# Middle stage's column products: three equal groups of frames, or 512, 512 and 128 with narrow matmuls between wide ones

## The chip, the cores and the metric

The kernel runs on one core of a Trainium2 chip. The metric is the device time of one execution in microseconds (us); lower is better. The core's engines work side by side and wait for each other by semaphores: TensorE (PE; its weight loads are shown apart as PEld), VectorE (DVE), ScalarE (ACT), GpSimd (POOL) and SyncE (SP), which here only issues DMAs. TensorE writes its sums to PSUM, eight banks of 512 float32 words in each of 128 partitions; DVE and ACT read them from there.

## The reference, cut to what matters

Two layers of a streaming encoder run for 1024 prompt frames and for 8 streams of 16 frames, T = 1152 frames together. Layer 0 is a gated linear recurrence. Between the layers its output projection, residual and LayerNorm give x (1152 x 1024). The second layer starts from x:

```python
def mla_queries(x, pos, w_in, q_norm_g, w_uq, w_uk):
    proj = jnp.einsum('btd,de->bte', x, w_in)      # 1024 -> 512 + 2048
    cq = rms_norm(proj[..., :Q_LORA], q_norm_g)    # Q_LORA = 512
    gate = proj[..., Q_LORA:]                      # used as o * silu(gate)
    ...
def shared_latent_kv(x, pos, w_dkv, kv_norm_g):
    kv = jnp.einsum('btd,de->bte', x, w_dkv)       # 1024 -> 256 + 64
```

The change is in how `proj` is computed. The matrix `w_in_b` has 512 + 2048 = 2560 columns, that is 20 tiles of 128: four of cq, sixteen of the gate.

## The kernel before, in words

float32 products are made from float32r operands in two parts: an operand is split into a high part (written by ACT, `round_high`, L104) and the rest (written by DVE, `round_low`, L109). A product is then three matmuls: high x low, low x high, high x high (`product`, L112 to L117). In the profile L115, L116 and L117 are these three matmuls for every stage of the kernel.

The middle stage (`middle_programs`, about 556 to 953 us) first finishes the first layer: for each of nine tiles of 128 frames, matmuls of 512 columns (`m_w`, `m_g`), a LayerNorm on DVE, eight transposes on TensorE (`turn_tile`, L1235), and the split of the turned tile into `act_h` (ACT) and `act_l` (DVE, semaphore `tl_done`, which starts at 1, so that tile t is there at t + 2). Then come the **column tiles**: for column tile i (i = 0 to 19, `NCOL`) 128 columns of `w_in_b` over all eight blocks of 128 inputs are the stationary operand, and the frames, `act_h` or `act_l`, are the moving one. A column tile is 3 groups of `TG` = 384 frames, each group 8 x 3 = 24 matmuls; so 72 matmuls of 384 columns for a tile and 1440 in all. Each group's sums stand in a bank of their own, 384 of its 512 words, and tile i uses banks 0 to 2 or 3 to 5 by turns (`pc`).

What sets the order around them:

- SP loads the float32 columns of tile i + 2 into `m_c_raw` (512 KB, L1127) once `c_done` has reached i + 1, that is once all matmuls of tile i are done. ACT makes `m_c_h` (`high_columns`), DVE makes `m_c_l` (`low_columns`, semaphore `cl_ready`), both buffers by turns of two.
- ACT reads the finished tile from PSUM: for the four cq tiles a Square (L1385) and a copy (L1386), for the gate tiles a Sigmoid (L1393), which DVE multiplies with the sums (L1509) and SP stores. TensorE may start tile i + 2 in the same banks after that (`columns_free`).
- The first two column tiles are begun before the last tile of frames is turned. Their order on TensorE is: tile 1's group 0, tile 0's group 0, `turn_tile(8)`, tile 0's groups 1 and 2, tile 1's groups 1 and 2. `c_done` is raised after group 2 of each: once for tile 0, once for tile 1. From tile 2 on, a tile's three groups follow each other.
- From gate tile 3 on, a transposition and a 128-frame product of the shared latent (`latent`, 24 matmuls of 320 columns, banks 6 and 7) follow each gate tile. After the last column tile the heads' programs (attention) follow on TensorE.

Of the kernel before, what the change touches and what calls it, by code (L numbers as in the profile page):

```python
# [9 lines left out]
ACT = mybir.ActivationFunctionType  # L10
# [5 lines left out]
KD = D // P  # L16
SEQ, NSEQ, SLEN, PAST = 1024, 8, 16, 1024
T = SEQ + NSEQ * SLEN
NT = T // P
NPB = SEQ // P  # L20
TG = 384
NTG = T // TG
# [9 lines left out]
BANK = 512  # L32


def flat(ap):
    return ap.rearrange("p a b -> p (a b)")
# [75 lines left out]
def product(nc, out, left, right, first, last):  # L112

    (lh, ll), (rh, rl) = left, right
    nc.tensor.matmul(out, ll, rh, start=first, stop=False)  # L115
    nc.tensor.matmul(out, lh, rl, start=False, stop=False)  # L116
    return nc.tensor.matmul(out, lh, rh, start=False, stop=last)  # L117

GLA_STEPS = ["V0", "V1", "K0", "C0", "S0", "SI", "O0", "K1", "C1", "S1", "O1", "OT0",
# [62 lines left out]
def rows_product(nc, bank, shared, i, t):  # L185

    gh, gl, _ = shared.tile_of(t)
    for h in range(2):
        cols = slice(h * BANK, (h + 1) * BANK)
        mm = product(nc, bank[:, h], (gh[:, i], gl[:, i]), (shared.w_h[i][:, cols], shared.w_l[i][:, cols]), i == 0, i == KD - 1)  # L190
    return mm
# [811 lines left out]
def middle_programs(nc, k, m, kept_at, heads):  # L1003
# [20 lines left out]
    cq_raw = Arena(nc, (cq_at, cq_at + 4 * 4 * T)).take("m_cq_raw", [4, T])  # L1024
# [21 lines left out]
    c_h = col.take("m_c_h", [2, KD, P], F32R)  # L1046
    c_l = col.take("m_c_l", [2, KD, P], F32R)
# [12 lines left out]
    sg = late.take("m_sg", [2, T])  # L1060
# [7 lines left out]
    bank = k.bank  # L1068

    def py(t):  # L1070

        b = (4, 0, 2, 6)[t] if t < 4 else (0, 2)[t % 2]
        return bank[:, b:b + 2]

    def pt(t):

        b = 6 if t and t % 2 == 0 else 4
        return bank[:, b:b + 2]

    def pc(i):  # L1080
        return bank[:, 3 * (i % 2):3 * (i % 2) + 3, 0:TG]

    w_loaded = [m.sem(f"m_w_loaded{i}") for i in range(nk)]
    g_loaded = [m.sem(f"m_g_loaded{i}") for i in range(2)]
# [18 lines left out]
    def columns_free(eng, i):  # L1103

        if i < NCQ:
            eng.wait_ge(cq_out, i + 1)
        else:
            eng.wait_ge(gate_out, i - NCQ + 1)
# [7 lines left out]
    def behind_gate(j):  # L1116

        t = j - 3
        return (t - 1 if 0 <= t - 1 < NPB else None), (t if 0 <= t < NT else None)
# [103 lines left out]
    @block.tensor  # L1223
    def _(pe):
        def turn_tile(t):

            pe.wait_ge(x_ready, t * 2 + 2)
            if t == 1:
                pe.wait_ge(tl_done, 2)
            elif t == 2:  # L1230
                pe.wait_ge(sum_done, 4)
            elif t > 2:
                pe.wait_ge(tl_done, t)
            for c in range(KD):
                last = nc.tensor.transpose(pt(t)[:, c // 4, (c % 4) * P:(c % 4 + 1) * P], x[t % 3][:, c * P:(c + 1) * P], k.ident[:])  # L1235
            last.then_inc(turned, 1)

        pe.sem_inc(y_done, 3)
        for t in range(3, NT):
            if t > 3:  # L1240
                pe.wait_ge(gl_ready, t - 3)
                pe.wait_ge(sum_done, t - 2 if t < 6 else t - 1)
            for kt in range(nk):
                last = rows_product(nc, py(t), sh, kt, t)
            last.then_inc(y_done, 1)
            if t < 7:
                turn_tile(t - 3)
            elif t == 7:
                turn_tile(4)
                turn_tile(5)  # L1250
            else:
                turn_tile(6)
                turn_tile(7)

        def columns(i, tg):

            cols = slice(tg * TG, (tg + 1) * TG)
            for kt in range(KD):
                mm = product(nc, pc(i)[:, tg], (c_h[:, i % 2, kt], c_l[:, i % 2, kt]),
                             (k.act_h[:, kt, cols], k.act_l[:, kt, cols]), kt == 0, kt == KD - 1)  # L1260
            if tg == NTG - 1:
                mm.then_inc(c_done, 1)

        pe.wait_ge(cl_ready, 2)
        pe.wait_ge(sum_done, 8)
        pe.wait_ge(tl_done, 4)
        columns(1, 0)
        pe.wait_ge(sum_done, 9)
        columns(0, 0)
        turn_tile(NT - 1)  # L1270
        pe.wait_ge(tl_done, 7)
        columns(0, 1)
        pe.wait_ge(tl_done, NT + 1)
        columns(0, 2)
        columns(1, 1)
        columns(1, 2)

        def column_tile(i):
            pe.wait_ge(cl_ready, i + 1)
            columns_free(pe, i - 2)  # L1280
            for tg in range(NTG):
                columns(i, tg)

        def spread_rows(tiles, b):

            for n, t in enumerate(tiles):
                mm = nc.tensor.transpose(bank[:, b, n * P:(n + 1) * P], sums[:, t * P:(t + 1) * P], k.ident[:])
            mm.then_inc(spread, 1)

        def latent(t):  # L1290
            if t == 0:
                pe.wait_ge(kvl_ready, 1)
            if t < 2:

                pe.wait_ge(spread_out, 2 + t)
            else:
                pe.wait_ge(tl_k, t - 1)
            for kt in range(KD):
                cols = slice(t * P, (t + 1) * P)
                mm = product(nc, bank[:, 6 + t % 2, 0:KV], (k.act_h[:, kt, cols], k.act_l[:, kt, cols]),  # L1300
                             (kvw_h[:, kt], kvw_l[:, kt]), kt == 0, kt == KD - 1)
            mm.then_inc(kv_done, 1)

        def turn_latent(t):
            b, par = bank[:, 6 + t % 2], t % 2
            pe.wait_ge(c_ready, t + 1)
            pe.wait_ge(kr_ready, t + 1)
            for c in range(2):
                nc.tensor.transpose(b[:, c * P:(c + 1) * P], cn[:, par, c * P:(c + 1) * P], k.ident[:])
            nc.tensor.transpose(b[:, 2 * P:3 * P], krn[:, par].rearrange("p a b -> p (a b)"), k.ident[:]).then_inc(turned_k, 1)  # L1310

        for i in range(2, NCQ):
            column_tile(i)
        for j in range(HEADS):
            column_tile(NCQ + j)
            if j == 0:
                pe.wait_ge(const_set, 3)
                pe.wait_ge(sums_step, NCQ - 1)
                for t in range(NT):
                    mm = nc.tensor.matmul(bank[:, 6, t:t + 1], sums[:, t * P:(t + 1) * P], ones[:], start=True, stop=True)  # L1320
                mm.then_inc(ss_done, 1)
            if j == 1:
                pe.wait_ge(rep_ready, 1)
                spread_rows(range(4), 7)
                spread_rows(range(4, 8), 6)
            if j == 2:
                pe.wait_ge(spread_out, 1)
                spread_rows(range(8, 9), 7)
            before, now = behind_gate(j)
            if before is not None:  # L1330
                turn_latent(before)
            if now is not None:
                latent(now)

    @block.scalar
    def _(act):
# [19 lines left out]
        def high_columns(i):  # L1356
            act.wait_ge(c_loaded[i % 2], 16 * (i // 2 + 1))
            if i >= 2:
                act.wait_ge(c_done, i - 1)
            round_high(nc, c_h[:, i % 2], c_raw[:, i % 2]).then_inc(ch_ready, 1)  # L1360
# [17 lines left out]
        def column_tile(i):  # L1378
            act.wait_ge(c_done, i + 1)
            if i < NCQ:  # L1380
                if i == 3:

                    act.wait_ge(sums_step, 1)
                dst = sums[:] if i == 0 else sg[:, i % 2]
                nc.scalar.activation(dst.rearrange("p (a b) -> p a b", a=3), pc(i), ACT.Square)  # L1385
                nc.scalar.copy(cq_raw[:, i].rearrange("p (a b) -> p a b", a=3), pc(i)).then_inc(cq_out, 1)  # L1386
            else:
                j = i - NCQ
                if j < 2:
                    act.wait_ge(sums_step, NCQ - 1)  # L1390
                else:
                    act.wait_ge(gate_stored[j % 2], 16 * (j // 2))
                nc.scalar.activation(sg[:, j % 2].rearrange("p (a b) -> p a b", a=3), pc(i), ACT.Sigmoid).then_inc(sig_done, 1)  # L1393
            if i + 2 < NCOL:
                high_columns(i + 2)

# [10 lines left out]
        for i in range(NCQ):  # L1407
            column_tile(i)
# [25 lines left out]
    def _(dve):  # L1434
# [69 lines left out]
        def column_tile(i):  # L1504
            if i >= NCQ:
                j = i - NCQ
                at = sg[:, j % 2].rearrange("p (a b) -> p a b", a=3)
                dve.wait_ge(sig_done, j + 1)
                nc.vector.tensor_tensor(at, pc(i), at, ALU.mult).then_inc(gate_out, 1)  # L1509
            if i + 2 < NCOL:  # L1510
                low_columns(i + 2)
# [41 lines left out]
        for i in range(NCQ):  # L1553
            column_tile(i)
# [1704 lines left out]
```

## Time and profile before

| | us |
|---|---|
| median of 3 runs | 1947.16 (1946.81 to 1948.17) |
| the profiled execution, its own time | 1946.45 |
| its span, first to last instruction | 1944.3 |
| busy in the span: PE / DVE / ACT / POOL | 1914.9 / 1061.8 / 768.6 / 394.0 |

A matmul's row in the trace gives its start and how long it took from there to its end. Matmuls overlap in their pipeline, so what a matmul costs TensorE is the step from its start to the next one's start, and not its duration. A row "x16" merges sixteen instructions: its duration reaches from the first start to the last end.

### The profile page before, as it was taken

Reading aid. Unit: us, or ns where it says so; the run is one execution under the profiler, and the core shown is the slowest. Engines: PE = TensorE matmul, PEld = TensorE weight load, DVE = VectorE, ACT = ScalarE, POOL = GpSimd, SP = SyncE. Lnnn points to the kernel's source line nnn. Section 1 sums busy time; section 2 is a strip of 40 time slices with the busy share of each in tenths; the row PEclk is TensorE's granted clock in tenths of the full one; section 3 lists DMA queues with packets and bytes.
Section 4 is the critical chain, followed back from the end, with each engine's and each line's share of the span. In section 5 each row is a group of like instructions: output and inputs, shape, how many; then the busy total and the mean of one; then the engine's idle time right before and its main releaser. Section 6 shows DMA issues by size and latency. Waiting matters only on the chain.

```text
span 1944.3 us, 31501 instructions
## 1 busy us (share of the span) xinstructions
PE 1914.9 (98%) x11771; PEld 1808.9 (93%) x11771; DVE 1061.8 (55%) x1943; ACT 768.6 (40%) x1346; POOL 394.0 (20%) x322
## 2 busy tenths in 40 slices
PE   9999999999999999999999999999999999999998
PEld 8999999999987999999999999999999989988886
DVE  4355446445658612422466676666666677753632
ACT  4333233233422221211455555555555567761100
POOL 0221222122311010000042432432433410000000
PEclk9999999999999999999999999999999999999999
DMA  6121122022236412233211112111111243363421
GB/s 183 34 78 55 35 67 78 27 62 68 79 117 201 128 44 69 80 107 104 89 34 50 41 50 63 34 54 56 38 49 42 73 135 92 96 226 136 157 87 43
DMA packets 186082, 158.55 MB, mean 82 GB/s; under 512 B 36144, under 2 KB 170544, under 8 KB 185744
## 3 DMA queue, kind: packets, MB, share of 16 engines
q1 hardware_dynamic: 180784, 139.60, 23.7%
q10 hardware_dynamic: 5040, 17.37, 2.6%
q8 instruction: 58, 0.95, 0.2%
q0 software_dynamic: 176, 0.43, 0.1%
q14 instruction: 24, 0.20, 0.0%
HBM read 115.52 MB, written 41.84 MB: 81 GB/s over the span
## 4 chain that ended last, share of the span: by engine, by line
PE 54%; DVE 7%; issue 5%; ACT 3%; DMA 1%; DVEq 0%; ACTq 0%; SPq 0%
PE ps L115 16%; PE ps L117 16%; PE ps L116 16%; PE ps L1925 1%; PE ps L1908 1%; PE ps L1907 1%; DVE h_pt_l L109 1%; ACT h_p L2041 1%; ACT h_p L2030 1%; DVE s_mx L2801 1%; DVE h_mx L2169 1%; DVE h_p L2126 1%; DVE h_p L2131 1%; DMA m_g_raw<-scratch_o 1%; DVE h_gate L2191 0%
## 5 line engine op out<-in xcount | busy, mean ns | idle before, releaser
L1821 POOL TENSOR_SCALAR h_p<-h_p,h_rsum 128x128 f32<-128x128 f32 (+7 forms) x128 | 220.7, 1725 | 442.8 <-DVE h_rsum L2173 442.8
L115 PE MATMUL ps<-act_h,a_w_l 128*128 128x384 f32 x768 | 270.8, 353 | 1.7 <-DVE a_w_l L109 1.7
L117 PE MATMUL ps<-act_h,a_w_h 128*128 128x384 f32 x768 | 260.1, 339 | 0.0
L116 PE MATMUL ps<-act_l,a_w_h 128*128 128x384 f32 x768 | 259.9, 338 | 0.0
L115 PE MATMUL ps<-act_h,m_c_l 128*128 128x384 f32 x480 | 162.9, 339 | 0.0
L117 PE MATMUL ps<-act_h,m_c_h 128*128 128x384 f32 x480 | 162.5, 339 | 0.0
L116 PE MATMUL ps<-act_l,m_c_h 128*128 128x384 f32 x480 | 162.5, 339 | 0.0
L115 PEld LDWEIGHTS ps<-act_h,a_w_l 128*128 128x128 f32 x768 | 144.2, 188 | 6.5 <-issue 3.3
L116 PEld LDWEIGHTS ps<-act_l,a_w_h 128*128 128x128 f32 x768 | 144.4, 188 | 3.3 <-issue 3.3
L117 PEld LDWEIGHTS ps<-act_h,a_w_h 128*128 128x128 f32 x768 | 144.1, 188 | 0.0
L104 ACT ACTIVATE h_pt_h<-ps 128x128 fp32r<-128x128 f32 (+2 forms) x192 | 87.1, 490 | 108.7 <-PE ps L1925 108.5
L109 DVE TENSOR_TENSOR h_pt_l<-ps,h_pt_h 128x128 fp32r<-128x128 f32 (+2 forms) x192 | 100.3, 551 | 47.8 <-ACT h_pt_h L104 47.8
L2041 ACT ACTIVATE h_p<-ps,h_mx 128x128 f32<-128x128 f32 (+7 forms) x128 | 94.8, 740 | 54.3 <-DVE h_mx L2169 54.0
L115 PE MATMUL ps<-o_w,o_g 128*128 128x512 f32 x288 | 112.4, 390 | 0.8 <-ACT s_olat L2677 0.8
L117 PE MATMUL ps<-o_w,o_g 128*128 128x512 f32 x288 | 112.1, 389 | 0.0
L116 PE MATMUL ps<-o_w,o_g 128*128 128x512 f32 x288 | 112.1, 389 | 0.0
L115 PE MATMUL ps<-cq_h,h_w_l 128*128 128x384 f32 x288 | 101.7, 353 | 0.6
L2169 DVE TENSOR_REDUCE h_mx<-ps 128x1 f32<-128x128 f32 (+7 forms) x128 | 97.0, 758 | 4.4
L117 PE MATMUL ps<-cq_h,h_w_h 128*128 128x384 f32 x288 | 96.5, 335 | 0.0
L116 PE MATMUL ps<-cq_l,h_w_h 128*128 128x384 f32 x288 | 96.4, 335 | 0.0
L115 PE MATMUL ps<-h_pt_h,h_v_l 128*128 128x256 f32 x320 | 92.3, 288 | 3.7 <-DVE h_gate L2191 3.0
L117 PE MATMUL ps<-h_pt_h,h_v_h 128*128 128x256 f32 x320 | 90.4, 283 | 0.0
(322 smaller groups left out, 4817.5 us busy)
## 6 DMA issues: line engine op xcount, KB each, us to landing
a_w_raw<-in_w_in_a SPq DMA_DIRECT2D x31, 512.0 KB, 4.1
m_c_raw<-in_w_in_b SPq DMA_DIRECT2D x20, 512.0 KB, 4.3
scratch_gate<-m_sg SPq DMA_DIRECT2D x16, 576.0 KB, 5.3
o_w_raw<-in_w_out_b SPq DMA_DIRECT2D x16, 512.0 KB, 6.3
h_gate<-scratch_gate SPq DMA_DIRECT2D x62, 128.0 KB, 2.0
scratch_og<-h_gate SPq DMA_DIRECT2D x62, 128.0 KB, 1.7
o_g_raw<-scratch_og SPq DMA_DIRECT2D x24, 256.0 KB, 4.3
a_xn<-in_x SPq DMA_DIRECT2D x9, 512.0 KB, 4.5
```

The source lines that it names most:

```text
L104: return nc.scalar.activation(high, x, ACT.Identity)
L109: return nc.vector.tensor_tensor(low, x, high.bitcast(F32), ALU.subtract)
L115: nc.tensor.matmul(out, ll, rh, start=first, stop=False)
L116: nc.tensor.matmul(out, lh, rl, start=False, stop=False)
L117: return nc.tensor.matmul(out, lh, rh, start=False, stop=last)
L1821: nc.gpsimd.tensor_scalar(weights_of(u), weights_of(u), rsum[:, u % PB], None, ALU.mult).then_inc(S["p_ready"], 1)
L1907: nc.tensor.matmul(out, rq[:, e, q], k.kr_l[:, kc], start=False, stop=False)
L1908: mm = nc.tensor.matmul(out, rq[:, e, q], k.kr_h[:, kc], start=False, stop=True)
L1925: mm = nc.tensor.transpose(bank[:, 4 + i % TB, j * P:j * P + P], p[:, u % PB, key * P:(key + 1) * P], k.ident[:])
L2030: last = nc.scalar.copy(rope_part(tg, 1)[b:b + 32], x[a:a + 32])
L2041: nc.scalar.activation(weights_of(u), scores_of(u), ACT.Exp, bias=mx[:, u % PB], accum_out=rsum[:, u % PB]).then_inc(S["exp_done"], 1)
L2169: nc.vector.tensor_reduce(mx[:, u % PB], scores_of(u), AX.X if n <= BANK else AX.XY, ALU.max, negate=True).then_inc(S["max_done"], 1)
```

## The change

The 1152 frames of a column tile are cut into 512, 512 and 128 instead of three times 384. The three banks then hold 1152 sums without holes (512, 512 and 128 words), and ACT and DVE read them as one run. The first group of 512 of a tile stands alone (24 matmuls). The second group of 512 and the group of 128 go side by side: for each input block and each of the three terms, first the matmul of 512 columns, then that of 128 columns with the same stationary operand. In the two tiles at the start, tile 1's second group goes side by side with the narrow groups of tile 0 and of tile 1: 512, 128, 128; and `c_done` is then raised by 2 at the end of this block. Two waits on `tl_done` ask for more turned tiles: 5 in place of 4 ahead of tile 1's group 0, and NT = 9 in place of 7 ahead of tile 0's group 1. The file gets 9 lines longer above this place, so that L1235 becomes L1244; the new matmuls are all L126.

```diff
+def products_beside(nc, parts, first, last):
+    for term in range(3):
+        for out, (lh, ll), (rh, rl) in parts:
+            mm = nc.tensor.matmul(out, lh if term else ll, rl if term == 1 else rh,
+                                  start=first and term == 0, stop=last and term == 2)
+    return mm
...
     def pc(i):
-        return bank[:, 3 * (i % 2):3 * (i % 2) + 3, 0:TG]
+        return flat(bank[:, 3 * (i % 2):3 * (i % 2) + 3])[:, 0:T]
...
-        def columns(i, tg):
-            cols = slice(tg * TG, (tg + 1) * TG)
+        def columns(*blocks):
             for kt in range(KD):
-                mm = product(nc, pc(i)[:, tg], (c_h[:, i % 2, kt], c_l[:, i % 2, kt]),
-                             (k.act_h[:, kt, cols], k.act_l[:, kt, cols]), kt == 0, kt == KD - 1)
-            if tg == NTG - 1:
-                mm.then_inc(c_done, 1)
+                parts = []
+                for i, tg in blocks:
+                    cols = slice(tg * BANK, min(tg * BANK + BANK, T))
+                    parts.append((pc(i)[:, cols], (c_h[:, i % 2, kt], c_l[:, i % 2, kt]),
+                                  (k.act_h[:, kt, cols], k.act_l[:, kt, cols])))
+                mm = products_beside(nc, parts, kt == 0, kt == KD - 1)
+            return mm
         pe.wait_ge(cl_ready, 2)
         pe.wait_ge(sum_done, 8)
-        pe.wait_ge(tl_done, 4)
-        columns(1, 0)
+        pe.wait_ge(tl_done, 5)
+        columns((1, 0))
         pe.wait_ge(sum_done, 9)
-        columns(0, 0)
+        columns((0, 0))
         turn_tile(NT - 1)
-        pe.wait_ge(tl_done, 7)
-        columns(0, 1)
+        pe.wait_ge(tl_done, NT)
+        columns((0, 1))
         pe.wait_ge(tl_done, NT + 1)
-        columns(0, 2)
-        columns(1, 1)
-        columns(1, 2)
+        columns((1, 1), (0, 2), (1, 2)).then_inc(c_done, 2)
         def column_tile(i):
             pe.wait_ge(cl_ready, i + 1)
             columns_free(pe, i - 2)
-            for tg in range(NTG):
-                columns(i, tg)
+            columns((i, 0))
+            columns((i, 1), (i, 2)).then_inc(c_done, 1)
```

The remaining lines of the diff take the `rearrange("p (a b) -> p a b", a=3)` off the operands of L1385, L1386, L1393 and L1509.

On TensorE, in the middle of any column tile from tile 2 on, there stands before (the names are moving and stationary operand):

```order
L115 MATMUL ps<-act_h,m_c_l 128x384
L116 MATMUL ps<-act_l,m_c_h 128x384
L117 MATMUL ps<-act_h,m_c_h 128x384
L115 MATMUL ps<-act_h,m_c_l 128x384
L116 MATMUL ps<-act_l,m_c_h 128x384
L117 MATMUL ps<-act_h,m_c_h 128x384
```

and now, where the tile's first group of 512 ends and the two other groups begin:

```order
L126 MATMUL ps<-act_h,m_c_l 128x512
L126 MATMUL ps<-act_l,m_c_h 128x512
L126 MATMUL ps<-act_h,m_c_h 128x512
L126 MATMUL ps<-act_h,m_c_l 128x512
L126 MATMUL ps<-act_h,m_c_l 128x128
L126 MATMUL ps<-act_l,m_c_h 128x512
L126 MATMUL ps<-act_l,m_c_h 128x128
L126 MATMUL ps<-act_h,m_c_h 128x512
```

Rows of 384 columns have become rows of 512, alone in the first third of a tile's matmuls and followed by a row of 128 in the rest.

On TensorE at the end of the block of tiles 0 and 1, where before the groups of 384 went one after the other, there stand now:

```order
L126 MATMUL ps<-act_h,m_c_h 128x512
L126 MATMUL ps<-act_h,m_c_l 128x512
L126 MATMUL ps<-act_h,m_c_l 128x128 x2
L126 MATMUL ps<-act_l,m_c_h 128x512
L126 MATMUL ps<-act_l,m_c_h 128x128 x2
L126 MATMUL ps<-act_h,m_c_h 128x512
L126 MATMUL ps<-act_h,m_c_h 128x128 x2
```

The last group of tile 0 has moved from ahead of tile 1's to beside it; both tiles are complete only with the last row of this block.

## Rows read from the trace of the kernel before

**Rows 1.** Page, engines' busy time in the whole span.
```profile
PE 1914.9 (98%) x11771; PEld 1808.9 (93%) x11771; DVE 1061.8 (55%) x1943; ACT 768.6 (40%) x1346; POOL 394.0 (20%) x322
```
**Rows 2.** Windows, all column tiles: length, busy time of engines, granted clock, DMA share, GB/s.
```profile
658.00:950.60 292.60, 292.60 (x1718) 292.20 (x1717) 84.24 (x141) 64.56 (x92) 20.21 (x25) 1.00 0.26 85
```
**Rows 3.** Waits of TensorE, 590 to 975 us: who for whom, us in total, times, longest.
```profile
PE ps L115 <- DVE m_x L1456: 2.4, 1, 2.4
```
**Rows 4.** Timeline of ACT, tiles 1 to 4: start, us, engine, line, out<-in, idle before.
```profile
684.62 1.13 ACT L1385 ACTIVATE m_sg<-ps 128x1152 f32<-128x1152 f32 x1 [3.61 <-PE ps L117]
...
722.78 1.13 ACT L1393 ACTIVATE m_sg<-ps 128x1152 f32<-128x1152 f32 x1 [7.93 <-PE ps L117]
```
**Rows 5.** Timeline of TensorE, stage of the first layer, one narrow between wide ones.
```profile
122.75 0.34 PE L117 MATMUL ps<-act_h,a_w_h 128*128 128x384 f32 x1
...
122.92 0.27 PE L438 MATMUL ps<-ident,a_on 128*128 128x128 f32 x1
122.93 0.19 PEld L115 LDWEIGHTS ps<-act_h,a_w_l 128*128 128x128 f32 x1
122.95 0.42 PE L115 MATMUL ps<-act_h,a_w_l 128*128 128x384 f32 x1
123.03 0.19 PEld L116 LDWEIGHTS ps<-act_l,a_w_h 128*128 128x128 f32 x1
123.21 0.34 PE L116 MATMUL ps<-act_l,a_w_h 128*128 128x384 f32 x1
```
**Rows 6.** Timeline of TensorE, one-column matmuls and the matmul behind them.
```profile
722.58 2.06 PE L1320 MATMUL ps<-m_ones,m_sums 128*128 128x1 f32 x18
...
724.59 0.19 PEld L116 LDWEIGHTS ps<-act_l,m_c_h 128*128 128x128 f32 x1
```
**Rows 7.** Timeline of TensorE, 512-column matmuls of the middle stage (first and last).
```profile
645.66 0.39 PE L116 MATMUL ps<-m_w_l,m_g_h 128*128 128x512 f32 x1
...
647.97 0.39 PE L117 MATMUL ps<-m_w_h,m_g_h 128*128 128x512 f32 x1
...
648.43 0.39 PE L116 MATMUL ps<-m_w_l,m_g_h 128*128 128x512 f32 x1
...
655.91 0.39 PE L116 MATMUL ps<-m_w_l,m_g_h 128*128 128x512 f32 x1
```
**Rows 8.** Timeline of TensorE, 384-column matmuls of the heads (first and last).
```profile
1116.18 0.34 PE L115 MATMUL ps<-cq_h,h_w_l 128*128 128x384 f32 x1
...
1117.22 0.33 PE L115 MATMUL ps<-cq_h,h_w_l 128*128 128x384 f32 x1
```
**Rows 9.** Timeline of DVE, turned tiles 4 and 5, 7, and 8.
```profile
645.82 2.36 DVE L109 TENSOR_TENSOR act_l<-ps,act_h 128x1024 fp32r<-128x1024 f32 x2 [2.81 <-ACT act_h L104]
...
665.13 1.21 DVE L109 TENSOR_TENSOR act_l<-ps,act_h 128x1024 fp32r<-128x1024 f32 x1
668.72 1.23 DVE L109 TENSOR_TENSOR act_l<-ps,act_h 128x1024 fp32r<-128x1024 f32 x1 [2.38 <-ACT act_h L104]
```
**Rows 10.** Timeline of all engines, from the end of tile 0 to tile 2's columns.
```profile
676.13 0.37 SPq L1127 DMA_DIRECT2D m_c_raw<-in_w_in_b  x1
...
679.95 1.06 ACT L104 ACTIVATE m_c_h<-m_c_raw 128x1024 fp32r<-128x1024 f32 x1 [1.58 <-DMA m_c_raw<-in_w_in_b]
681.04 1.23 DVE L109 TENSOR_TENSOR m_c_l<-m_c_raw,m_c_h 128x1024 fp32r<-128x1024 f32 x1 [7.26 <-ACT m_c_h L104]
```
**Rows 11.** DMA issues, 590 to 700 us: out<-in, queue, count, size, us to landing.
```profile
m_g_raw<-scratch_o SPq DMA_DIRECT2D x1, 1024.0 KB, 8.6
```
**Rows 12.** Timeline of TensorE, the last matmul of the kernel.
```profile
1935.46 0.39 PE L117 MATMUL ps<-o_w,o_g 128*128 128x512 f32 x1
```
**Rows 13.** Windows behind it, columns as in rows 2.
```profile
1940.00:1941.00 1.00, 0.00 (x0) 0.00 (x0) 0.34 (x1) 0.00 (x0) 0.00 (x0) 0.84 0.45 170
1941.00:1942.00 1.00, 0.00 (x0) 0.00 (x0) 0.00 (x0) 0.00 (x0) 0.00 (x0) 0.50 0.95 354
```
**Rows 14.** Timeline of TensorE at the kernel's start.
```profile
1.32 3.78 PE L589 MATMUL ps<-a_sct 128*128 128x128 f32 x16 [1.32 <-POOL a_sct L722]
```

More of the change, by code:

```diff
@@ L1384, in column_tile @@
                 dst = sums[:] if i == 0 else sg[:, i % 2]
-                nc.scalar.activation(dst.rearrange("p (a b) -> p a b", a=3), pc(i), ACT.Square)
-                nc.scalar.copy(cq_raw[:, i].rearrange("p (a b) -> p a b", a=3), pc(i)).then_inc(cq_out, 1)
+                nc.scalar.activation(dst, pc(i), ACT.Square)
+                nc.scalar.copy(cq_raw[:, i], pc(i)).then_inc(cq_out, 1)
             else:
@@ L1392, in column_tile @@
                     act.wait_ge(gate_stored[j % 2], 16 * (j // 2))
-                nc.scalar.activation(sg[:, j % 2].rearrange("p (a b) -> p a b", a=3), pc(i), ACT.Sigmoid).then_inc(sig_done, 1)
+                nc.scalar.activation(sg[:, j % 2], pc(i), ACT.Sigmoid).then_inc(sig_done, 1)
             if i + 2 < NCOL:
@@ L1506, in column_tile @@
                 j = i - NCQ
-                at = sg[:, j % 2].rearrange("p (a b) -> p a b", a=3)
+                at = sg[:, j % 2]
                 dve.wait_ge(sig_done, j + 1)
```

## The prediction

> **What bounds the kernel now.** I read the page's busy times first: TensorE is busy for 1914.9 of 1944.3 us, every other engine for 55% at most [rows 1]. So a change on TensorE goes to the end one to one, unless the stage where it stands has a wait on TensorE that could shrink. Second, the window over all column tiles: 292.6 of 292.6 us busy at the full granted clock, DVE 84 us, ACT 65 us, DMA 26% [rows 2]. Third, the waits: from 590 to 658 us one of 2.4 us, on a LayerNorm [rows 3], and none within the column tiles, which rows 2 also say. A busy TensorE is not one at its peak, so fourth the timeline, where the step between matmul starts is the cost. Between the ends of tiles 1 and 4 lie 722.78 - 684.62 = 38.16 us [rows 4], for three tiles of 72 matmuls: 12.72 us a tile, 0.1767 us a matmul of 384 columns. At the full clock of 2.4 GHz the columns alone are 0.160 us. There is thus about 0.017 us a matmul over the columns, and the change trades in that: as many matmuls (1440) and as many columns, cut in another way.
>
> **The cost of a matmul by its width.** 512 columns: 33 steps from 648.43 to 655.91 are 0.2267 us each; ten steps from 645.66 to 647.97 are 0.231 [rows 7]. 384 columns: in the heads 6 steps in 1.04 us, 0.1733 [rows 8]; here 0.1767. From 384 to 512 the cheaper values differ by 0.0534 us, the time of 128 columns at 2.4 GHz, so that a wide matmul costs its columns and 0.0133 us. The same stationary and moving tensors cost 2% over that line here, and I carry this over: 512 columns at 0.230 us, with 0.2267 and 0.2325 as ends.
>
> 128 columns: the line would give 0.067 us. The rows say otherwise. In the first layer's stage a single transposition of 128 columns stands between 384-column matmuls: from L117 at 122.75 to L116 at 123.21 there are 0.46 us for one wide, the narrow and one wide; less twice 0.1767 that is 0.107 us for the narrow one [rows 5]. The weight loads show why. The load for the wide L115 starts at 122.93, when the narrow matmul starts and not before, and L115 gets the array at 123.03, when the following load starts. Only one set of weights is loaded ahead, and loading it takes about 0.11 us whatever streams beside it. Eighteen matmuls of one column take from 722.58 to 724.59, where the next wide one takes over: 0.112 us each [rows 6]. So a narrow matmul costs the load of the *next* matmul's weights, and a wide one beside it, with 0.12 us to spare, can't take that over. I take 0.110 us, bounds 0.107 and 0.112. These rows are of plain float32 transpositions and one-column products, but what waits behind them is a float32r load like those here.
>
> **The Trainium skill** on this: "TensorE: Matmul & The Clock Gate", Part 2, on the back-to-back issue gap, puts the sustained cost of pairs of weight load and matmul at 81 ns for 128 columns, and explains it by weight loads pulled ahead in a 64-deep window. With 0.081 in place of 0.110, and all else as below, the sum would be 14 us lower. The rows go against it here: one load ahead, 0.107 to 0.112 us.
>
> **Part 1, the cut into 512, 512, 128.** A tile is now 24 x (0.230 + 0.230 + 0.110) = 13.68 us against 12.72: +0.96 us, and for 20 tiles +19.2 us. Tiles 0 and 1 have the same four groups of 512 and two of 128 between them, so they count alike. Bounds: 24 x (2 x 0.2267 + 0.107) = 13.45, +14.6 us in all; 24 x (2 x 0.2325 + 0.112) = 13.85, +22.6.
>
> **Part 2, the banks without holes.** ACT's and DVE's reads are of 1152 elements before and after; one takes 1.13 us and has idle time of 7.9 us before it [rows 4]. Faster or slower by any plausible share, nothing reaches TensorE: nil.
>
> **Part 3, the waits on turned tiles.** `tl_done` 5 is reached long before 658 us, since the tiles 4 and 5 are through at 648.2. `tl_done` 9 needs DVE's turned tile 7, which ends at 666.3 [rows 9]. The new tile 0, group 1 comes at 658.1 + 48 x 0.230 + eight transposes of 0.11 = 670.0: 3.7 us of cover. Turned tile 8 follows the transposes, which now come at 669.1 in place of 666.6: done on DVE at about 672.5, wanted at 675.5. Nil, with 3 us of cover. `turn_tile(8)` also lets ACT go on to the split of the latent's weights, 2.5 us later than before; they are first used behind gate tile 3, five tiles on.
>
> **Part 4, the shared end of tiles 0 and 1.** This is a new wait. Before, tile 0 was complete at 676.1, and SP issued the load for tile 2 at once; it was split by ACT from 679.95 and by DVE from 681.04 to 682.27 [rows 10], while TensorE worked on tile 1, whose end released ACT at 684.62 [rows 4]. That chain is 682.27 - 676.13 = 6.14 us, and it had 2.3 us to spare. Now `c_done` goes from 0 to 2 only at the end of the block: 675.5 + 24 x (0.230 + 2 x 0.110) = 686.3. Behind that instant stands the whole chain, for SP's L1127 waits for `c_done` 1. TensorE's `column_tile(2)` waits for `cl_ready` 3, and all of TensorE is queued behind it: 6.1 us of idle time and 0.2 to 0.3 for the drained pipeline, 6.4 us. ACT's Square and copy of tile 0 (2.2 us from the same instant) fit into the load's 3.8 us. Two loads of 512 KB are now issued together, and one of 1024 KB took 8.6 us with others around it [rows 11]: the upper bound is 4.8 us more. Below, nothing: no load can begin before the block's end. Tile 3 isn't late: its parts are there at about 696 us, wanted at 706. From then on each tile has 13.7 us for a 7 us chain.
>
> **Part 5, the clock.** The last matmul ends at 1935.46 + 0.39 = 1935.85 [rows 12]; the granted clock's mean is 0.84 between 1940 and 1941 and 0.50 after [rows 13], so it fell to 1.2 GHz at about 1940.7, after 4.8 us without a matmul. The idle time of part 4 is longer. TensorE would then start tile 2 at the low level. What coming back costs stands at the kernel's start: sixteen 128-column matmuls take 3.78 us [rows 14], about 0.23 us a step, twice what they cost later. At half speed 3.6 us of work lose 1.8. I add 1.8 us, bounds 0 and 3.
>
> **Sum.** 19.2 + 6.4 + 1.8 = 27.4 us on the profiled 1946.45: 1973.9. That execution lies 0.7 us under the median of the runs, inside their spread. Low ends 14.6 + 6.2 + 0 = 20.8, 1967; high ends 22.6 + 11.2 + 3 = 36.8, 1983. Nothing behind gives it back: the heads follow on TensorE directly, and TensorE waits there for parts of a us. I forecast **1974 us**.
>
> **Rivals.**
>
> *Weights further ahead (11%).* The fp32r loads of this stream run two ahead, or the narrow matmul, which has its neighbour's weights, needs no load. Then it costs what the line gives, 0.1767 less 256 columns (0.1067), 0.070 us. A tile is 24 x 0.530 = 12.72: no change, and parts 4 and 5 remain: +8.2, 1954.7. For it speaks that wide loads leave 0.12 us free; against it, rows 5 and 6, and the page's count of as many weight loads as matmuls, though L116 and L117 share their stationary operand [rows 1]. (It is the mechanism that the Trainium skill describes in the section cited above; by its 81 ns the time would be 1960.)
>
> *The faster one (3%).* The 0.0133 us over the columns are the price of handing over, and a narrow matmul directly behind a wide one with the same weights doesn't pay them: 0.0534. With wide ones at 0.2267 a tile is 24 x 0.5068 = 12.16, -11.1 us for 20; with the 8.2 of parts 4 and 5 that is -2.9: 1943.6. It decides if a wide, a wide and a narrow together cost less than 0.5300 - 8.2/480 = 0.513 us. Its place would be the second part of each tile. Against it: the narrow matmul of rows 5 is right behind a wide one and costs double.
>
> *A longer stall (10%).* The two loads land together like one of 1 MB: +4.8 on the forecast, 1979. Against it: the load wanted first is also issued first, and alone it took 3.8 us [rows 10].
>
> *Smaller variants, within the forecast's 76%.* If the clock stays up, 1972; if the wide ones cost 0.2267 too, 1968.
>
> **Numbers.** Likeliest, 76%: 1974, its own range 1966 to 1980. The range for 8 in 10 is 1960 to 1981: it leaves out the first two rivals and part of the high bounds. A difference within 0.2% (3.9 us) of before can't be told from none. Slower 0.94: forecast, long stall and nearly all of the first rival. Same 0.03: the first rival with every bound low (0.0667 and 0.2267 give -4.6, the stall +6.4). Faster 0.03.
>
> **What would show it.** In the timeline of the changed kernel, a wide and a narrow L126 in turn: starts 0.23 and 0.11 us apart, the wide one's weight load starting with the narrow matmul. ACT's rows of successive tiles 13.7 us apart. One wait of TensorE of about 6 us on DVE's `m_c_l` near 686 us, a granted clock of 0.5 at its end. L1136 issued twice in a row at 686. Wrong: pairs of 0.30 us, tiles of 12.7 us; no wait at 686; or a new wait ahead of tile 0's group 1.

## The result, and the profile after

The changed kernel takes 1978.39 us, the median of 4 runs (1977.55 to 1979.54), against 1947.51 (1946.81 to 1948.17) before: ratio 1.016, 95% interval 1.0148 to 1.0173. It is slower by 30.9 us. The forecast was 1974, 26.5 us over this median of before, in a range of 1960 to 1981.

The page's busy times, beside [rows 1]: the same instructions, TensorE busy 26 us longer in a span of 1976.3 us, 32.0 us longer.

```profile
PE 1941.2 (98%) x11771; PEld 1791.9 (91%) x11771; DVE 1063.1 (54%) x1943; ACT 768.4 (39%) x1346; POOL 394.5 (20%) x322
```

ACT's rows on the finished column tiles 2, 3, 4, 5 and 19 show where the time goes, beside [rows 4] (start, us, engine, line, operation, idle time before it and its releaser):

```profile
709.16 1.14 ACT L1394 ACTIVATE m_sg<-ps 128x1152 f32<-128x1152 f32 x1 [14.94 <-PE ps L126]
723.00 1.14 ACT L1394 ACTIVATE m_sg<-ps 128x1152 f32<-128x1152 f32 x1 [9.12 <-PE ps L126]
736.84 1.13 ACT L1402 ACTIVATE m_sg<-ps 128x1152 f32<-128x1152 f32 x1 [9.02 <-PE ps L126]
754.25 1.13 ACT L1402 ACTIVATE m_sg<-ps 128x1152 f32<-128x1152 f32 x1 [12.54 <-PE ps L126]
...
982.83 1.14 ACT L1402 ACTIVATE m_sg<-ps 128x1152 f32<-128x1152 f32 x1 [11.67 <-PE ps L126]
```

and two of the kernel before, tiles 2 and 19:

```profile
697.34 1.13 ACT L1385 ACTIVATE m_sg<-ps 128x1152 f32<-128x1152 f32 x1 [7.98 <-PE ps L117]
...
950.87 1.14 ACT L1393 ACTIVATE m_sg<-ps 128x1152 f32<-128x1152 f32 x1 [10.55 <-PE ps L117]
```

Tile 2 is 11.8 us late, tile 19 32.0 us, and the span no more than that: all of it is lost in the column tiles, and nothing behind gives any back. A tile is 13.84 us now, +1.12. (In the eight tiles where the latent's products stand between, the step from ACT's row to the next is 17.64 us against 16.57, +1.07.) The step from 736.84 to 754.25 is 17.41 us; with the eighteen one-column matmuls of 0.112 us that stand there, 15.87 were due, as run 1 below has it.

The timeline of TensorE within the pairs (PEld rows are weight loads; "x2" merges a wide and a narrow matmul, or their loads):

```profile
703.81 0.51 PE L126 MATMUL ps<-act_h,m_c_l 128*128 128x512 f32 x2
703.87 0.19 PEld L126 LDWEIGHTS ps<-act_h,m_c_l 128*128 128x128 f32 x1
704.10 0.30 PEld L126 LDWEIGHTS ps<-act_l,m_c_h 128*128 128x128 f32 x2
704.16 0.51 PE L126 MATMUL ps<-act_l,m_c_h 128*128 128x512 f32 x2
...
705.53 0.51 PE L126 MATMUL ps<-act_h,m_c_h 128*128 128x512 f32 x2
```

Five pairs from 703.81 to 705.53 are 0.344 us each. The merged row of two loads lasts 0.30 us and a single load 0.19, so the second starts 0.11 us after the first. The loads start 0.23 and 0.11 us apart by turns (703.87, 704.10, 704.21); the rows of the matmuls start 0.29 and 0.06 us apart (703.81, 704.10, 704.16), so within a pair they don't show what each one costs. The load for the next wide matmul starts with the narrow matmul's row, at 704.10. The groups of 512 that stand alone step 0.2333 us (15 steps here):

```profile
709.49 0.39 PE L126 MATMUL ps<-act_h,m_c_h 128*128 128x512 f32 x1
...
712.99 0.39 PE L126 MATMUL ps<-act_h,m_c_h 128*128 128x512 f32 x1
```

So a narrow matmul adds 0.344 - 0.233 = 0.11 us. The handover of tiles 0 and 1, beside [rows 10], all engines:

```profile
686.37 0.99 SPq L1136 DMA_DIRECT2D m_c_raw<-in_w_in_b  x2
686.46 1.13 ACT L1394 ACTIVATE m_sums<-ps 128x1152 f32<-128x1152 f32 x1 [13.26 <-PE ps L126]
...
690.18 1.06 ACT L104 ACTIVATE m_c_h<-m_c_raw 128x1024 fp32r<-128x1024 f32 x1 [1.58 <-DMA m_c_raw<-in_w_in_b]
...
691.27 1.23 DVE L109 TENSOR_TENSOR m_c_l<-m_c_raw,m_c_h 128x1024 fp32r<-128x1024 f32 x1 [15.22 <-ACT m_c_h L104]
...
692.55 0.80 PE L126 MATMUL ps<-act_h,m_c_l 128*128 128x512 f32 x1 [6.21 <-DVE m_c_l L109]
```

Both loads are issued at 686.37, the splits follow in turn, and TensorE waits 6.21 us. The windows around it and around the one-column matmuls (length, busy time of PE, PEld, DVE, ACT, POOL, granted clock, DMA share, GB/s):

```profile
687.00:688.00 1.00, 0.00 (x0) 0.00 (x0) 0.00 (x0) 1.00 (x2) 0.00 (x0) 0.95 0.26 74
688.00:689.00 1.00, 0.00 (x0) 0.00 (x0) 0.00 (x0) 0.60 (x1) 0.00 (x0) 0.50 1.06 313
...
697.00:698.00 1.00, 1.00 (x4) 0.81 (x3) 0.08 (x1) 0.00 (x0) 0.00 (x0) 0.50 0.00 0
698.00:699.00 1.00, 1.00 (x6) 0.82 (x5) 0.00 (x0) 0.00 (x0) 0.00 (x0) 0.93 0.00 0
...
738.00:739.00 1.00, 1.00 (x9) 0.95 (x10) 0.99 (x1) 0.00 (x0) 0.00 (x0) 1.00 0.84 240
739.00:740.00 1.00, 1.00 (x4) 0.79 (x3) 0.36 (x1) 0.00 (x0) 0.00 (x0) 0.55 0.89 268
...
742.00:743.00 1.00, 1.00 (x4) 0.82 (x4) 1.00 (x2) 0.00 (x0) 0.00 (x0) 0.75 0.00 0
```

The clock is at its lower level (1.2 GHz) from 687.9 to 698.1 us; TensorE works again from 692.6, so it works at half speed for 5.6 us. It is low once more from 739.1 to 742.5, where TensorE is never idle. That second stretch was not forecast.

### The profile page after: what moved, and what is told of

Read it like the earlier page. It is cut to its first block, busy times and chain, and to the rows that moved or that the text cites. A ratio compares the mean times of both kernels' runs of the same rounds, so it can differ in the third digit from the quotient of the medians.

```text
span 1976.3 us, 31501 instructions
## 1 busy us (share of the span) xinstructions
PE 1941.2 (98%) x11771; PEld 1791.9 (91%) x11771; DVE 1063.1 (54%) x1943; ACT 768.4 (39%) x1346; POOL 394.5 (20%) x322
## 4 chain that ended last, share of the span: by engine, by line
PE 55%; DVE 6%; issue 4%; ACT 3%; DMA 1%; DVEq 0%; ACTq 0%; SPq 0%
PE ps L126 14%; PE ps L115 12%; PE ps L117 11%; PE ps L116 11%; PE ps L1934 1%; PE ps L1917 1%; PE ps L1916 1%; DVE h_pt_l L109 1%; ACT h_p L2050 1%; DVE s_mx L2810 1%; DVE h_mx L2178 1%; ACT h_p L2039 1%; DVE h_p L2135 1%; DMA m_g_raw<-scratch_o 1%; DVE h_p L2140 1%
## 5 line engine op out<-in xcount | busy, mean ns | idle before, releaser
L126 PE MATMUL ps<-act_h,m_c_l 128*128 128x512 f32 (+1 forms) x480 | 145.5, 357 | 6.2 <-DVE m_c_l L109 6.2
L126 PE MATMUL ps<-act_h,m_c_h 128*128 128x512 f32 (+1 forms) x480 | 146.1, 359 | 0.0
L126 PE MATMUL ps<-act_l,m_c_h 128*128 128x512 f32 (+1 forms) x480 | 145.7, 358 | 0.0
L126 PEld LDWEIGHTS ps<-act_h,m_c_l 128*128 128x128 f32 x480 | 81.2, 191 | 21.3 <-DVE m_c_l L109 6.4
L1518 DVE TENSOR_TENSOR m_sg<-ps,m_sg 128x1152 f32<-128x1152 f32 x16 | 21.7, 1358 | 139.9 <-ACT m_sg L1402 139.9
```

Of the source, the lines that this page charges most:

```text
L126: mm = nc.tensor.matmul(out, lh if term else ll, rl if term == 1 else rh, start=first and term == 0, stop=last and term == 2)
```

## The experiments

**1. Tile 0 and tile 1 end apart.** In the changed kernel:

```diff
-        columns((1, 1), (0, 2), (1, 2)).then_inc(c_done, 2)
+        columns((0, 2)).then_inc(c_done, 1)
+        columns((1, 1), (1, 2)).then_inc(c_done, 1)
```

> The changed kernel's cut (512, 512, 128), but tile 0 is finished first and raises c_done by itself, then tile 1: group 2 of tile 0 goes alone ahead of the pair of groups of tile 1. Same matmuls, same count. If the wait at 686 us comes from the shared end alone, it is gone, and with it the low clock behind it (5.5 us at half the clock, 2.5 us lost): 1978.4 - 6.4 - 2.5 = 1969.5 us, ratio to before 1.011. Rival: the wait comes from the 512-column groups making everything later, and stays near 6 us: 1978. The second low stretch (739.4 to 742.5 us, 1.6 us lost) should go too if it depends on the moment at which the one-column matmuls fall, and stay if narrow matmuls in a row cause it every time.

Measured: 1968.87 us, ratio to before 1.0111 (1.0094 to 1.0128). From 650 to 1010 us TensorE's only wait is one of 1.3 us in the heads; the one at 686 us is gone, and the granted clock is 1.00 throughout the column tiles (658 to 978 us). ACT's rows of tiles 0, 1 and 2:

```profile
680.67 1.13 ACT L1395 ACTIVATE m_sums<-ps 128x1152 f32<-128x1152 f32 x1 [5.06 <-PE ps L126]
688.83 1.14 ACT L1395 ACTIVATE m_sg<-ps 128x1152 f32<-128x1152 f32 x1 [3.54 <-PE ps L126]
702.67 1.14 ACT L1395 ACTIVATE m_sg<-ps 128x1152 f32<-128x1152 f32 x1 [9.17 <-PE ps L126]
```

Tile 0 is done 8.2 us before tile 1, more than the chain of 6.1 us. The shared end, with all that hangs on it, is worth 1978.39 - 1968.87 = 9.5 us; the other 21.3 us over before are the cut itself, 1.07 a tile (22.0 us by the profile: twelve tiles at 1.12 and eight at 1.07). By the profiles, from the end of tile 1 to that of tile 19, the shared end is worth 10.4 us. Part of the difference can come from elsewhere: in this run's profile the clock was low ahead of the changed stage, behind a wait on a LayerNorm that ends at 597.7:

```profile
599.00:600.00 1.00, 1.00 (x4) 0.80 (x3) 0.96 (x3) 0.54 (x1) 0.75 (x2) 0.50 1.09 376
```

Such a stretch, from about 598 to 601.5 us, stands in the profiles of runs 1, 4, 5 and 7 and not in the others, of the kernel before and of the changed one among them. It comes and goes ahead of anything that the change touches. Run 4 shows its price: tiles 0 and 1 end there 1.5 us later than in the changed kernel.

**2. The shared end alone, on the kernel before.**

```diff
-            if tg == NTG - 1:
-                mm.then_inc(c_done, 1)
+            if tg == NTG - 1 and i != 0:
+                mm.then_inc(c_done, 2 if i == 1 else 1)
```

> The kernel before with its 384-column groups, and one edit: c_done isn't raised after tile 0 but by 2 after tile 1. Nothing else of the change. Theory (the wait is the chain load, split, split behind the shared end): one wait of TensorE of 6.2 us at 684.6 us, then a stretch at half the clock that costs 2.5 us: 1947.5 + 8.9 = 1956.4. Rival (the wait needs the new cut as well, or the clock stays up): 1947.5 to 1954.

Measured: 1954.99 us, 7.4 over before (ratio 1.0045, 1.0028 to 1.0061). One new wait, in TensorE's list from 650 to 1010 us, and the clock low behind it:

```profile
PE ps L115 <- DVE m_c_l L109: 6.3, 1, 6.3
```

```profile
692.00:693.00 1.00, 1.00 (x5) 1.00 (x5) 0.74 (x1) 0.23 (x1) 1.00 (x1) 0.50 0.00 0
...
694.00:695.00 1.00, 1.00 (x7) 1.00 (x6) 1.00 (x1) 0.00 (x0) 0.01 (x1) 0.89 0.00 0
```

The wait needs nothing of the new cut. Work began again at 690.6 and the clock rose at 694.2, after 3.7 us and not 5.5 as in the changed kernel: some 1.8 us lost. With the wait that is 8.1, within the interval of the measured difference (5.5 to 11.9). The time alone hardly tells this from the rival's 1954; the wait and the low clock in the profile do.

**3. Narrow groups behind the wide ones, not beside them.**

```diff
-            columns((i, 1), (i, 2)).then_inc(c_done, 1)
+            columns((i, 1))
+            columns((i, 2)).then_inc(c_done, 1)
```

and in the first block (1, 1), (0, 2), (1, 2) one after the other.

> The changed kernel with the narrow groups not beside the wide ones but behind them: 24 matmuls of 512, 24 of 512, 24 of 128 in each tile (in the first block 512, 128, 128 one after the other). Same count, same shared end. Theory (one load of weights ahead, 0.110 us each, wherever the narrow matmul stands): no change, 1978.4 within 1 us, tile 13.84 us. Rival (the alternation hides part of the narrow ones' weight loads under the wide ones, which have 0.12 us to spare): slower by up to 480 x 0.04 = 19 us, 1990 and more.

Measured: 1979.83 us (ratio to before 1.0173, 1.0156 to 1.019), 1.4 over the changed kernel with overlapping intervals. ACT's rows of two tiles, and the last narrow matmuls of tile 3 (14 steps of 0.111 us from 721.23):

```profile
709.23 1.13 ACT L1397 ACTIVATE m_sg<-ps 128x1152 f32<-128x1152 f32 x1 [14.90 <-PE ps L126]
723.11 1.13 ACT L1397 ACTIVATE m_sg<-ps 128x1152 f32<-128x1152 f32 x1 [9.22 <-PE ps L126]
```

```profile
721.23 0.27 PE L126 MATMUL ps<-act_h,m_c_l 128*128 128x128 f32 x1
...
722.79 0.28 PE L126 MATMUL ps<-act_h,m_c_h 128*128 128x128 f32 x1
```

A tile is 13.88 us against 13.84. The alternation saves 0.04 us a tile, 0.8 us in all: nearly nothing of the narrow matmul's price is hidden by the wide neighbour.

**4. 32 columns in place of 128.** The last 96 frames are left incomplete from the second input block on.

```diff
                     cols = slice(tg * BANK, min(tg * BANK + BANK, T))
+                    if tg == 2 and kt:
+                        cols = slice(2 * BANK, 2 * BANK + 32)
```

> The changed kernel with the narrow matmuls 32 columns wide in place of 128 from the second input block on (the last 96 frames are left incomplete). Theory (the narrow one costs the next weight load, not its columns): no change, 1978.4 within 1 us, pair 0.343 us. Rival (its columns count: 96 columns are 0.040 us at 2.4 GHz): 420 x 0.040 = 16.8 us less, 1961.6, pair 0.303 us.

Measured: 1976.55 us, 1.8 under the changed kernel. Its profile also has another clock: no second low stretch (1.5 us less), 1.2 us less lost behind the wait, and 1.5 us more at 598 us. So the narrow matmuls are better read from the rows. A tile is 13.77 us against 13.84, which is 1.3 us in all, and five pairs take 1.70 us:

```profile
704.87 0.49 PE L126 MATMUL ps<-act_h,m_c_h 128*128 128x512 f32 x2
...
706.57 0.49 PE L126 MATMUL ps<-act_l,m_c_h 128*128 128x512 f32 x2
```

0.340 us a pair against 0.344: three quarters of the narrow matmuls' columns were worth 0.004 us and not 0.040. The price isn't that of its columns, and it is as long as the step between two weight loads, 0.11 us.

**5. 448, 448, 256, with two ends.** Each group in its own bank, the last two side by side; ACT and DVE read a tile in two instructions.

```diff
-                    cols = slice(tg * BANK, min(tg * BANK + BANK, T))
-                    parts.append((pc(i)[:, cols], ...
+                    cols = slice(tg * 448, min(tg * 448 + 448, T))
+                    parts.append((bank[:, 3 * (i % 2) + tg, 0:cols.stop - cols.start], ...
...
-        columns((1, 1), (0, 2), (1, 2)).then_inc(c_done, 2)
+        columns((0, 2)).then_inc(c_done, 1)
+        columns((1, 1), (1, 2)).then_inc(c_done, 1)
```

> As the run with two ends, but cut 448, 448, 256, the last two side by side; each group in a bank of its own, so ACT and DVE read a tile in two instructions. All groups are now wide enough that their columns (256: 0.107 us) reach about the weight load's time. Theory (a matmul costs its columns and 0.013 us, but never less than a weight load of 0.110; here with 0 to 0.007 us more, as the 384 and 512 ones of this operand): 24 x (0.200 + 0.200 + 0.107 + 3 x 0.0133 + 0.01) = 12.77 us a tile against 12.72 before: 1947.6 to 1949 us, same as before. Rival (unequal groups side by side cost something of their own, whatever their width): above 1952.

Measured: 1946.27 us, before 1946.22 in the same set of runs, ratio 1.0002 (0.9992 to 1.0011): no difference. Eleven steps of 448 columns, here the first two rows, are 0.2045 us each:

```profile
713.72 0.36 PE L126 MATMUL ps<-act_l,m_c_h 128*128 128x448 f32 x1
713.92 0.37 PE L126 MATMUL ps<-act_h,m_c_h 128*128 128x448 f32 x1
```

Fifteen pairs from 716.62 to 721.52 are 0.327 us each, so a matmul of 256 columns costs 0.122 us. A tile is 12.76 us against 12.72. A cut whose narrowest group is 256 columns costs what three equal groups cost, within the noise: unequal groups have no price of their own that shows here, and no profit.

**6 and 7. Which operand makes a 512-column matmul 0.2333 us.** As 1, but the wide groups move the tile's own columns (6), or the stationary operand is taken from the frames (7). Neither computes the stage's products any more.

```diff
-                                  (k.act_h[:, kt, cols], k.act_l[:, kt, cols])))
+                                  (k.act_h[:, kt, cols], k.act_l[:, kt, cols]) if tg == 2 else
+                                  (flat(c_h[:, i % 2, 4:8]), flat(c_l[:, i % 2, 4:8]))))
```

> As the run with two ends, but the groups of 512 take their moving operand from the tile's own columns (m_c_h, m_c_l, 512 of them, the same for all input blocks) and not from the frames, which leaves the products wrong. Question: why a matmul of 512 columns steps 0.2333 us here and 0.2267 elsewhere. If it is where the moving operand lies or how it is strided: 0.2267, and 960 x 0.0066 = 6.3 us less than with two ends, 1962.6. If it is the stationary operand, the banks written or the stage: 0.2333, 1968.9.

```diff
-                    parts.append((pc(i)[:, cols], (c_h[:, i % 2, kt], c_l[:, i % 2, kt]),
+                    parts.append((pc(i)[:, cols], (k.act_h[:, kt, 0:P], k.act_l[:, kt, 0:P]),
...
```

> As the run with two ends, but the stationary operand is taken from the frames (act_h, act_l, first 128) and not from m_c_h and m_c_l; the moving one stays as it is. The products are wrong. If the stationary operand's place makes the 0.2333: 0.2267, 1962.6. If the moving one's: 0.2333, 1968.9. With the run before this one: both at 0.2333 would leave banks or the stage, both at 0.2267 that the two operands meet in the same place.

Measured: 1968.96 and 1966.86 us, one run each. The wide matmuls that stand alone step 0.227 us in both, seven steps in run 6 and twelve in run 7:

```profile
714.29 0.39 PE L126 MATMUL ps<-m_c_h 128*128 128x512 f32 x1
...
715.88 0.39 PE L126 MATMUL ps<-m_c_h,m_c_l 128*128 128x512 f32 x1
```

```profile
703.72 0.39 PE L126 MATMUL ps<-act_h 128*128 128x512 f32 x1
...
706.44 0.39 PE L126 MATMUL ps<-act_h 128*128 128x512 f32 x1
```

But a tile falls only to 13.76 and to 13.64 us. In run 6 the pairs are no cheaper than in the changed kernel (0.3465 us, twenty of them from 706.84 to 713.77), in run 7 hardly (0.341). So neither operand alone makes the 0.2333, and "the two meet in one place" doesn't fit either, since they share a tensor where the step is short. Two different tensors aren't enough for it: `m_w` and `m_g` step 0.2267 [rows 7]. Nor is `act` in the stationary place: in the kernel before, the latent's 320-column matmuls with `m_kvw` moving and `act` stationary step 0.147 us, their columns (0.1333) and 0.013. Among the long streams of the kernel before, the surcharge shows only where `act` moves and another tensor is stationary, in the first layer's stage too (0.1767 us for 384 columns with `a_w`). The cause of these 0.0066 us stays open.

**8. Four times as many one-column matmuls,** in the kernel of experiment 1, whose clock had stayed up.

```diff
-                for t in range(NT):
+                for t in 4 * list(range(NT)):
```

> As the run with two ends (in whose profile the clock stayed up), with the eighteen one-column matmuls behind gate tile 0 done four times over: 72 in place of 18, 0.112 us each, results the same. Question: whether the second stretch at the low clock, 739.4 to 742.5 us in the changed kernel, comes from matmuls that keep TensorE's queue busy but its array nearly empty. If so: the granted clock falls to 0.50 near these matmuls, although TensorE has no idle time, and the run costs 54 x 0.112 = 6.0 us and some 2 to 6 us more. Rival (only idle time lets the clock fall, and the second stretch was the echo of the first): clock 1.00 throughout, 6.0 us more, 1974.9.

Measured: 1979.93 us, one run, with the clock low:

```profile
727.90 11.11 PE L1330 MATMUL ps<-m_ones,m_sums 128*128 128x1 f32 x72
```

```profile
732.00:733.00 1.00, 1.00 (x10) 1.00 (x9) 0.26 (x1) 0.70 (x1) 0.00 (x0) 0.83 0.00 0
733.00:734.00 1.00, 1.00 (x7) 1.00 (x6) 0.96 (x1) 0.00 (x0) 0.00 (x0) 0.50 0.00 0
...
742.00:743.00 1.00, 1.00 (x4) 0.80 (x3) 0.52 (x1) 0.00 (x0) 0.00 (x0) 0.55 0.00 0
```

The clock fell with TensorE busy in every window: a busy TensorE alone doesn't keep it up. ACT's rows of tiles 4 and 5 stand 26.68 us apart; the tile (13.84) and the 72 matmuls (8.06) are 21.9, so the low clock cost 4.8 us. With the 54 further matmuls (6.0 us) that is 10.8 us more than run 1, and the two times differ by 11.1. The rival, that only idle time lets the clock fall, is out.

**9. The changed kernel once more.**

> The changed kernel once more, unaltered, for its profile. If the second low stretch is a matter of the moment, it may be absent (span 1.6 us shorter than 1976.3); if the layout of the work makes it, it stands at 739 us again. The first one, behind the wait at 686 us, has to be there either way, but may begin earlier or later than 1.8 us after the last matmul.

Measured: 1978.19 us. Both low stretches are there again, from 690.6 to 697.4 and from 738.4 to 741.8:

```profile
690.00:691.00 1.00, 0.00 (x0) 0.00 (x0) 0.00 (x0) 0.91 (x1) 0.00 (x0) 0.81 1.19 289
...
738.00:739.00 1.00, 1.00 (x6) 0.91 (x6) 1.00 (x1) 0.00 (x0) 0.00 (x0) 0.70 1.04 310
```

The first one began 2.7 us later than in the first profile, in the same wait.

## Why the prediction was right

- **The cut (part 1).** Right in mechanism, low by 2 to 3 us. Forecast +0.96 us a tile and +19.2 in all; measured +1.12 a tile, and 21.3 us by the runs of experiment 1 (22.0 by the profile). The term that was mis-sized is the wide matmul: 0.2333 us, where I had carried over a 2% surcharge for this operand and rounded it to 0.230; it lies just above the upper bound, 0.2325. The narrow one is the 0.110 us forecast. Runs 3 and 4 bear out what the prediction made of it: it costs the same among its like as beside wide ones, and 96 columns fewer change 0.004 us. That a single set of weights is loaded ahead fits these steps, but no row shows it directly. The sign expected, matmul starts 0.23 and 0.11 us apart, came in the rows of the weight loads and not in those of the matmuls. By the 81 ns of the Trainium skill ("TensorE: Matmul & The Clock Gate", Part 2, back-to-back issue gap) the sum would, as an estimate, have been 14 us lower; the rows go against it: the narrow matmul adds 0.11 us here, and 0.107 even at 32 columns.
- **The holes (part 2), the waits on turned tiles (part 3).** Nil, as forecast: no wait of TensorE stands ahead of tile 0's group 1.
- **The shared end (part 4).** Forecast 6.1 us of idle time, measured 6.21, and 6.3 with the old cut (run 2). The two loads in one issue were not slower: ACT's split began 3.8 us behind the issue, as before, so that the rival of a longer stall falls.
- **The clock (part 5).** The direction was right, the reasoning in part luck. I took the time to the fall, 4.8 us, from the kernel's end; here it came 1.6 us after the last matmul in one profile (686.3 to 687.9), and 4.5 us after it in the other (686.16 to 690.62); in runs 3, 4 and 2 it was 1.4, 2.5 and 3.2. The 4.8 us were thus at the long end, and a wait of 6.2 was longer than any. The 3.6 us of work at half speed that the loss was worked out from stand in no row (the nearest has 3.78, [rows 14]); they were 5.6 us here, 5.0 in run 9, 3.7 in run 2. The loss: tile 2 runs from 692.7 (second weight load) to ACT's row at 709.16, 16.4 us for what takes 13.84 and 0.3 for the last matmul's end elsewhere, so 2.3 us against 1.8 forecast.
- **What the prediction lacked** is the second low stretch, 17.41 - 15.87 = 1.5 us. The clock fell 2.5 us after the start of the eighteen one-column matmuls, which in [rows 6] went by at full clock. They come after 24 pairs in which TensorE streams 640 columns in 0.344 us, against 768 in 0.353 before. Whether that is why the clock fell isn't settled: of the seven with narrow pairs or groups, five have it (the changed kernel twice, runs 3, 6 and 7) and two don't (1 and 4); of the three with 384 or 448 (before, 2, 5) none has.
- **The rivals.** Weights further ahead (1954.7) and the free narrow matmul (1943.6) both needed a narrow matmul of 0.07 us or less, and fall with runs 3 and 4. Two small sums in this part are off and carry nothing: the variant with the clock up and wide ones at 0.2267 is 1969, not 1968, and the low bounds of the first rival give -4.75, not -4.6.

The ledger in the profile's terms: 12 x 1.12 + 8 x 1.07 = 22.0, the wait with the drained pipeline 6.4, the low clock 2.3 and 1.5: 32.2 against 32.0 us in the span. The forecast's sum was 27.4: low in the cut and in the clock, right in the wait, and no error made up for another.

## What to carry to other kernels

In these runs a matmul that has its own weight load costs its columns at 2.4 GHz and 0.013 to 0.020 us, but not less than the step between two weight loads, about 0.11 us: 0.2333 us for 512 columns, 0.2045 for 448, 0.1767 for 384, 0.122 for 256, and still 0.11 for 128 and 0.107 for 32. So width saved in one matmul is no time given to its neighbour, and where the count of matmuls stays the same, as here, equal groups are as good as any. 256 columns were wide enough and 128 were not; no width between them was tried, nor was another count of matmuls. Where two units of work are made to end together, look at what each end released: here the first one started the next unit's load, and joining them laid a chain of 6 us bare.

## What the runs showed of the hardware that was not expected

- The granted clock fell to 1.2 GHz with TensorE busy without a gap: at 732.7 us, 4.8 us into 72 one-column matmuls, and stayed low for 10 us, into the wide ones behind them (experiment 8).
- In the wait of 6.2 us behind the shared end it fell 1.6 us after the last matmul in one profile of the changed kernel and 4.5 us after it in another; over all profiles with this wait the time lies between 1.4 (run 3) and 4.5 us.
- Behind the wait on a LayerNorm at 595 us, 2.4 to 2.8 us long in all profiles, the clock is low for 3.4 us in four profiles (runs 1, 4, 5 and 7) and stays up in the seven others. The kernel's time moves by some 1.5 us with it, without any change to its code.
- A 512-column matmul with `act` moving and `m_c` stationary steps 0.2333 us, 448 columns 0.2045, 384 columns 0.1767; with both operands from one tensor, or `m_w` moving and `m_g` stationary, 512 columns take 0.227. Over columns at 2.4 GHz this is 0.020, 0.018 and 0.017 us. Neither operand by itself explains it.
